# Where an expert's tokens sit among its slots, and the order of the last expert's loads and of the last sums

## The reference, cut to what matters

```python
scores = sigmoid(x @ w_router)                  # 544 x 64
idx = top_k(group_limited(scores + b_router), 6)
wts = scores[idx] / sum(scores[idx]) * 2.5
routed[token] += wts * (silu(x @ w_gate[e]) * (x @ w_up[e])) @ w_down[e]
shared = (silu(x @ ws_gate) * (x @ ws_up)) @ ws_down
out = layer_norm(ALPHA * x + routed + shared)
```

## Time and profile before

| | |
|---|---|
| median of 3 executions | 1910.4 us |
| the profiled execution, its own time | 1910.4 us |
| its span, first to last instruction | 1908.6 us |
| mean granted TensorE clock | 0.964 |
| TensorE busy | 1764.4 us, 92% of the span |
| VectorE / ScalarE / GpSimd busy | 748.9 / 552.0 / 346.0 us |
| moved by DMA | 358.60 MB |

### The profile page before, as it was taken

The page is one execution under the profiler, slowest core; times in us unless marked ns, Lnnn a source line. Parts: engine busy times, 40 slices in busy tenths (PEclk is TensorE's granted clock), DMA queues, the critical chain, the costliest instruction groups (busy, mean ns, idle before and its releaser), DMA issues. The chain is left out here.

```text
span 1908.6 us, 26693 instructions
## 1 busy us (share of the span) xinstructions
PE 1764.4 (92%) x10107; PEld 1168.1 (61%) x10107; DVE 748.9 (39%) x1853; ACT 552.0 (29%) x1293; POOL 346.0 (18%) x360
## 2 busy tenths in 40 slices
PE   8999999999999989899888788998999888899987
PEld 6577777777777768788666655565444344344432
DVE  1044544454554310265887443264222222222215
ACT  2134234233333321365667333020111111111110
POOL 0011211211211120031554262001111111111100
PEclk9999999999999989899799899999999999999999
DMA  7061221231232243153000365806999999999968
GB/s 234 1 215 47 64 75 47 57 82 47 57 73 54 46 118 95 45 177 94 14 2 1 133 214 186 302 26 274 364 421 420 420 420 419 419 421 419 419 272 321
DMA packets 165360, 358.60 MB, mean 188 GB/s; under 512 B 36920, under 2 KB 114736, under 8 KB 140400
## 3 DMA queue, kind: packets, MB, share of 16 engines
q1 hardware_dynamic: 144880, 295.33, 42.1%
q0 software_dynamic: 19872, 60.31, 8.9%
q10 hardware_dynamic: 480, 1.25, 0.2%
HBM read 337.75 MB, written 35.31 MB: 195 GB/s over the span
## 5 line engine op out<-in xcount | busy, mean ns | idle before, releaser
L848 PE MATMUL bank<-xT,arena 128*128 128x272 f32 x1440 | 373.1, 397 | 0.0
L848 PEld LDWEIGHTS bank<-xT,arena 128*128 128x128 f32 x1440 | 256.8, 190 | 58.1 <-issue 16.8
L2726 PE MATMUL bank<-arena,kvt 128*64 128x512 f32 (+1 forms) x816 | 263.9, 624 | 30.8 <-issue 29.9
L2726 PEld LDWEIGHTS bank<-arena,kvt 128*64 128x64 f32 (+1 forms) x816 | 89.9, 150 | 167.3 <-issue 167.3
L1265 POOL TENSOR_TENSOR arena<-arena 128x512 f32<-128x512 f32 x48 | 56.7, 1182 | 435.7 <-DVE arena L1355 261.3
L2805 PE MATMUL bank<-arena,kvt 128*64 128x512 f32 (+1 forms) x408 | 128.1, 598 | 2.4 <-issue 2.1
L3126 DVE SCALAR_TENSOR_TENSOR kvt<-kvt,arena,bank 128x256 f32<-128x256 f32 x37 | 17.8, 480 | 259.2 <-ACT kvt L2916 259.2
L2726 PE MATMUL bank<-xT,kvt 128*64 128x512 f32 (+1 forms) x208 | 99.6, 635 | 11.2 <-issue 11.2
L2572 POOL DMA_INDIRECT hT<-x_rows,rows_i x37 | 37.6, 1017 | 375.0 <-DVE rows_i L3057 375.0
L2916 ACT ACTIVATE kvt<-bank 128x256 f32<-128x256 f32 x37 | 14.2, 384 | 296.5 <-PE bank L2726 296.5
L1621 PE MATMUL bank<-xT,arena 128*128 128x272 f32 x352 | 83.0, 400 | 8.6 <-PEq L163 8.6
(11 more groups left out here) (504 smaller groups left out, 2994.9 us busy)
## 6 DMA issues: line engine op xcount, KB each, us to landing
arena<-in_w_exp_gate SPq DMA_DIRECT2D x51, 1024.0 KB, 21.7
arena<-in_w_exp_up SPq DMA_DIRECT2D x51, 1024.0 KB, 25.5
arena<-in_w_exp_down SPq DMA_DIRECT2D x51, 1024.0 KB, 24.6
arena<-in_w_in SPq DMA_DIRECT2D x48, 512.0 KB, 5.3
kvt<-in_w_exp_down SPq DMA_DIRECT2D x13, 1024.0 KB, 24.3
xT<-in_w_exp_gate SPq DMA_DIRECT2D x13, 1024.0 KB, 22.7
xT<-in_w_exp_up SPq DMA_DIRECT2D x13, 1024.0 KB, 26.2
arena<-y_rows SPq DMA_DIRECT2D x9, 1024.0 KB, 18.5
```

Of the source, the lines that this page charges most:

```text
L848: last = mm(banks[2 * (i % 2) + half][:, 0:HALF], wh[blk % RING][:, k, :], xT[:, k, half * HALF:(half + 1) * HALF], start=(k == 0), stop=( ...
L2726: last = mm(banks[2 + 4 * (t % 2)][cols, :], xgT[:, k, cols], ewgu[i % EBUF][:, :, k], start=(k == 0), stop=(k == KD - 1))
```

## The change

Three things are changed.

1. The constants `places_one` and `places_pair` and their two loads are gone. `match` compares with `slots`, whose value at slot s is s + 1: the list numbers lie in the slots in order, and the empty slots are the last ones of each expert. The two waits on `r_in` count 112 instead of 144.
2. The loads of the last two experts: one wait (for the gate_up of turn 34), then gate of 62, gate of 63, up of 62, up of 63 on two semaphores, then one wait for `y_banked` and both down matrices. In the last turn TensorE computes all gate columns first, after waiting for the gate matrices alone, and then all up columns after waiting for the up matrices: 32 calls of 256 columns instead of 16 of 512.
3. The last sums: `shared_down(3)` is moved ahead of the first chunk, and `shared_down(4)` with its wait stands behind `add_rows(3)` instead of ahead of it.

```diff
-            sp.dma_start(places_one, io["places_one"]).then_inc(r_in, 16)
-            sp.dma_start(places_pair, io["places_pair"]).then_inc(r_in, 16)
...
-            both = [(i, bass.ds(sp.value_load(...), 1)) for i in (NE - 2, NE - 1)]
-            for i, which in both:
-                sp.wait_ge(gu_banked, TURN_OF[i - EBUF] + 1)
-                load_gate_up(sp, i, which)
-            for i, which in both:
-                sp.wait_ge(y_banked, TURN_OF[i - EBUF] + 1)
+            both = [bass.ds(sp.value_load(...), 1) for i in (NE - 2, NE - 1)]
+            sp.wait_ge(gu_banked, TURN_OF[NE - 1 - EBUF] + 1)
+            for m, (name, landed) in enumerate((("w_exp_gate", last_gate_in), ("w_exp_up", last_up_in))):
+                for i, which in zip((NE - 2, NE - 1), both):
+                    sp.dma_start(ewgu[i % EBUF][:, m], io[name][0, which].rearrange("o (p k) n -> p (o k) n", p=P)).then_inc(landed, 16)
+            sp.wait_ge(y_banked, TURN_OF[NE - 1 - EBUF] + 1)
+            for i, which in zip((NE - 2, NE - 1), both):
                 load_down(sp, i, which)
...
             def gate_up(t):
-                for _, i, _ in columns(t):
-                    pe.wait_ge(we_in[i % EBUF], 32 * (i // EBUF + 1))
+                if t < NTURN - 1:
+                    for _, i, _ in columns(t):
+                        pe.wait_ge(we_in[i % EBUF], 32 * (i // EBUF + 1))
...
+                if t == NTURN - 1:
+                    for m, landed in enumerate((last_gate_in, last_up_in)):
+                        pe.wait_ge(landed, 32)
+                        for k in range(KD):
+                            for _, i, cols in columns(t):
+                                last = mm(banks[2 + 4 * (t % 2)][cols, m * DE:m * DE + DE], xgT[:, k, cols], ewgu[i % EBUF][:, m, k], start=(k == 0), stop=(k == KD - 1))
...
-            for q in range(3):
+            for q in range(4):
                 shared_down(q)
             pe.wait_ge(sums_in, 16)
             add_sample()
-            add_rows(1)
-            shared_down(3)
-            add_rows(2)
-            pe.wait_ge(sum_saved, 2)
-            shared_down(4)
-            add_rows(3)
-            add_rows(4)
+            for q in range(1, NTILE):
+                if q == 4:
+                    pe.wait_ge(sum_saved, 2)
+                    shared_down(q)
+                add_rows(q)
...
-                    last = V.tensor_tensor(onehot[t % 2][:, :, cols], (places_pair if len(TURNS[t]) == 2 else places_one).rearrange(...).to_broadcast([P, NTILE, width]),
+                    last = V.tensor_tensor(onehot[t % 2][:, :, cols], slots[:, 0:width].rearrange(...).to_broadcast([P, NTILE, width]),
                                            pos[:, :, which].to_broadcast([P, NTILE, width]), ALU.is_equal)
```

More of the change, by code:

```diff
@@ L121, in shape_constants @@
     c["slots"] = np.broadcast_to(i + 1, (P, P)).astype(f)
[L122 to L125, removed]
     c["runs"] = np.broadcast_to(np.arange(NTILE * NE) % NE != 0, (P, NTILE * NE)).astype(f)
@@ L435, in build @@
         slots = d(P)
-        places_one = d(P)
-        places_pair = d(LIGHT)
         capb = d(NE)
@@ L2431, in build @@
         chunk_in = [sem(f"chunk_in{i}") for i in range(14)]
+        last_gate_in = sem("last_gate_in")
+        last_up_in = sem("last_up_in")
         sums_in = sem("sums_in")
@@ L2524, in _ @@
                 load_down(sp, i, which)
-            both = [(i, bass.ds(sp.value_load(order[0:1, RANKS[i]:RANKS[i] + 1], min_val=0, max_val=NE - 1), 1)) for i in (NE - 2, NE - 1)]
-            for i, which in both:
-                sp.wait_ge(gu_banked, TURN_OF[i - EBUF] + 1)
-                load_gate_up(sp, i, which)
-            for i, which in both:
-                sp.wait_ge(y_banked, TURN_OF[i - EBUF] + 1)
+            both = [bass.ds(sp.value_load(order[0:1, RANKS[i]:RANKS[i] + 1], min_val=0, max_val=NE - 1), 1) for i in (NE - 2, NE - 1)]
+            sp.wait_ge(gu_banked, TURN_OF[NE - 1 - EBUF] + 1)
[4 more added lines that the diff above has]
+            for i, which in zip((NE - 2, NE - 1), both):
                 load_down(sp, i, which)
@@ L2656, in logits @@
                 if t == 0:
-                    pe.wait_ge(r_in, 144)
+                    pe.wait_ge(r_in, 112)
                 for k in range(KD):
@@ L2723, in gate_up @@
                     pe.wait_ge(h_ready, t - 1)
-                for k in range(KD):
-                    for _, i, cols in columns(t):
-                        last = mm(banks[2 + 4 * (t % 2)][cols, :], xgT[:, k, cols], ewgu[i % EBUF][:, :, k], start=(k == 0), stop=(k == KD - 1))
+                if t == NTURN - 1:
[4 more added lines that the diff above has]
+                                last = mm(banks[2 + 4 * (t % 2)][cols, m * DE:m * DE + DE], xgT[:, k, cols], ewgu[i % EBUF][:, m, k], start=(k == 0), stop=(k == KD - 1))
+                else:
+                    for k in range(KD):
+                        for _, i, cols in columns(t):
+                            last = mm(banks[2 + 4 * (t % 2)][cols, :], xgT[:, k, cols], ewgu[i % EBUF][:, :, k], start=(k == 0), stop=(k == KD - 1))
                 last.then_inc(gu_banked, 1)
@@ L3046, in match @@
                     width = cols.stop - cols.start
-                    last = V.tensor_tensor(onehot[t % 2][:, :, cols], (places_pair if len(TURNS[t]) == 2 else places_one).rearrange("p (o s) -> p o s", o=1).to_broadcast([P, NTILE, width]),
+                    last = V.tensor_tensor(onehot[t % 2][:, :, cols], slots[:, 0:width].rearrange("p (o s) -> p o s", o=1).to_broadcast([P, NTILE, width]),
                                            pos[:, :, which].to_broadcast([P, NTILE, width]), ALU.is_equal)
@@ L3067, in _ @@
                 norm(t)
-            dve.wait_ge(r_in, 144)
+            dve.wait_ge(r_in, 112)
             step(V.tensor_copy(R[:, :, 0], tokens[:, :, 0:1].to_broadcast([P, NTILE, NE])))
```

## The result

The change makes the kernel slower by 1.0%: 1929.22 us (median of 6 executions, 1926.38 to 1931.8) against 1909.51 us before (6 executions, 1909.12 to 1912.25), a ratio of 1.0101 with the interval 1.0088 to 1.0113. The profiled execution took 1931.04 us; its span is 1929.2 us, 20.6 us more than the one before.

A forecast was written before the change was run, and what follows sets the result against it. The prediction took the DMA transfers to bound the expert turns; 18.4 + 1.9 + 0.3 + 0.3 + 0 = 20.9 us on a span of 1908.6, with 1.8 around it, gave 1931.3 us, range 1918 to 1938.

The forecast's parts named there:

- Part 1: Expert turns: slots in order keep one DMA engine's eight slots filled, so turn 35 starts 18.4 us later.
- Lower bound 14.0, eight neighbours: Slot order, expert turns: if each engine serves eight neighbouring partitions, 14.0 us; within the smaller-imbalance rival, chance 0.10.
- Colder clock in turn 35: Turn 35's gate_up: a longer wait before it brings a slower clock and 9.0 us, +1.9 us, bounds 0 and 3.0.
- Part 2: Last two experts' loads and split gate_up: at most a 0.34 us wait saved, gate_up 7.10 to 7.8; taken +0.3 us.
- leaves no hole: Later issue of the last experts' loads: the queue still holds 11.4 us of work, so no delay.
- Last scatter: Scatter before the reading back: 7 rows on the fullest engine instead of 5, +0.3 us.
- Part 3: Reordered last sums: the wait before VectorE's group 4 only changes owner, 0 us, bounds -1.3 and +1.
- The signs: Expected traces: full-stretch share about 0.97, about 400 GB/s, gate_up waits up 15 to 20 us, weights landing in 22 us or more.
- Common limit: Rival, expert turns: memory limits all engines together, full ones speed up when light ones idle; 1912.5 us, chance 0.04.
- nothing: Rival, gathers and scatters: share-out is not by partition, so slot order does nothing; 1910.4 + 0.3 us, chance 0.02.
- faster: Rival, gathers and scatters: rows dealt one slot at a time, fullest engine falls by 15.4 us; 1895 us, chance 0.03.
- More: Rival, end of expert turns: turn 36's later loads meet an empty queue or cold clocks add up; +3 to +8 us, chance 0.06.

The follow-up runs named there:

- e1: Kernel before with only the list numbers in slot order and both constants gone, loads and sums as before: 1931.88 us against 1910.83, ratio 1.0118.
- e4: Kernel before with other constants: every second group of four slots wants the lower half of the list, the others the upper: 1935.95 us, ratio 1.0133.
- e5: Kernel before with other constants: slots 0 to 31 of each 64 want the lower half of the list, the rest the upper: 1910.06 us, ratio 0.9994.
- e9: Kernel before with slots 0-3 and 32-35 of each 64 holding list numbers 1 to 8, others dealt evenly: 1925.28 us, ratio 1.0103.
- e12: Kernel before with slots 24-27 and 56-59 of each 64 always filled, others dealt evenly: 1930.43 us against 1906.93, one execution.
- e14: Kernel before with slots 16-19 and 48-51 of each 64 always filled, others dealt evenly: 1933.96 us against 1906.93, one execution.
- e6: Kernel before with list numbers in reversed order, so the empty slots come first: 1933.72 us, ratio 1.0143.
- e13: Kernel before with slots 28-31 and 60-63 of each 64 always filled, others dealt evenly: 1924.82 us against 1906.93, one execution.
- e10: Kernel before with the groups of four mirrored within each 32 slots in every second pair of experts: 1906.52 us, ratio 1.0004.

## Why the prediction was right

The median came at 1929.2 us, 2.1 below the forecast, and the term that carries the forecast came for its reason. That the total is so near is in part luck: of the 20.6 us in the profile 4.7 were lost before turn 1, where the change does nothing, and what lies behind turn 1 adds up to 15.9 us against 20.9 forecast. Point by point:

**Part 1, +18.4 at turn 35.** Measured 17.2 over the expert stretch (e1: 16.7). The step that carries it, 62 transfers with 8 full slots on one engine times 0.156 us for a row, was right in kind: fixed groups (e4 against e5), fullest engine alone (e9). Its size was 1.2 us too large. The 378 rows before were read from the drain, and the count gives the same; but what the base is remains open, since the even variants differ in their fullest engine and not in time. Against the count of 495 to 378, 117 rows, the 17.2 us make 0.147 us a row.

**The assumption that engines are alike** stood in that step unsaid, and it is wrong (e12, e14). It did no harm because the change fills slots 0 to 7 and leaves the slow groups less full, by my count 392 rows on the engine of 16 to 19 and 308 on that of 24 to 27. With the full slots at 24 to 27 the same sum would have fallen 7 us short.

**Lower bound 14.0, eight neighbours.** Refuted by e4 and e5. The two ideas put the changed kernel's fullest engine at the same rows (496 against 495), because the first 36 slots are full either way, and differ only in the base, 14.0 against 18.4 us; that is why the two ideas could be left side by side in the forecast, and why other edits were needed to tell them apart.

**Colder clock in turn 35, +1.9.** Not in the profiled execution: turn 34 was itself late there and the wait before turn 35 was 2.71 us, followed by 7.10. It is in e1 (3.86, then 9.88), e4, e6, e9, e12, e13 and e14, but also in e10, whose engines are even (3.18, then 10.10), so it does not hang on the longer wait alone. So the term is real in some executions and absent in others, and the medians can't be parted into it. The rule that it came from, a wait of 3.5 us and the next gate_up takes 8.5, was too sharp. In e10 a wait of 4.02 us came before a gate_up of 7.10, and in the kernel before one of 3.01 came before 8.78. In the kernel after a wait of 2.24 us came before a gate_up of 8.79, one of 3.25 before 10.04, and one of 2.71 before 7.10.

**Part 2, +0.3.** Measured -0.3 from turn 35 to turn 36 in the profile. SyncE's queue in the kernel after:

```profile
1839.12 0.34 SPq L2524 DMA_DIRECT2D arena<-in_w_exp_gate  x1
1839.65 0.33 SPq L2524 DMA_DIRECT2D xT<-in_w_exp_gate  x1
1840.08 0.38 SPq L2524 DMA_DIRECT2D arena<-in_w_exp_up  x1
1840.55 0.63 SPq L2524 DMA_DIRECT2D xT<-in_w_exp_up  x1
1844.84 0.81 SPq L552 DMA_DIRECT2D arena<-in_w_exp_down  x2
```

All four go after turn 34's gate_up, as described, and turn 36 does not suffer: the down product of turn 35 ends and gate_up starts at once, at 1860.48. But "leaves no hole" was wrong for the lightly loaded engines. They stood mostly idle before the four loads came, while turn 35 still waited for its weights from the full ones; in e1, which issues the loads of expert 62 earlier, they did not. The kernel after, then e1:

```profile
1832.00:1836.00 4.00, 4.00 (x20) 1.36 (x20) 0.64 (x1) 0.55 (x1) 1.01 (x1) 1.00 0.63 258
1836.00:1840.00 4.00, 4.00 (x23) 1.80 (x19) 0.48 (x1) 0.38 (x1) 0.00 (x0) 1.00 0.29 119
```

```profile
1832.00:1836.00 4.00, 3.66 (x16) 1.26 (x16) 0.07 (x1) 0.10 (x2) 0.00 (x0) 1.00 0.97 399
1836.00:1840.00 4.00, 0.25 (x2) 0.28 (x4) 0.62 (x1) 0.53 (x1) 0.99 (x1) 0.82 1.02 426
```

From 1840 to 1856 us the share in the kernel after is back at 0.99 to 1.02. The hole cost nothing that the stretch shows (+17.2 here, +16.7 in e1), since turn 35 waits for the full engines. The 0.34 us wait of the earlier trace rows is saved, as the working had it for a warm turn 35. The finer matmuls cost nothing: 6.92 us for 64 of them, against 7.10 for 32, so the range of 7.10 to 7.8 lay on the wrong side.

**Last scatter, +0.3.** Measured 3.49 us against 4.79, a gain of 1.3 in this pair of profiles; e1 with the same slots took 4.30. What drains ahead of it differs between the kernels, and one landing was too little to put 0.3 on.

**Part 3, 0.** Measured +0.5, within -1.3 to +1. The wait has changed its owner as described. VectorE in the kernel after, end of group 3 and start of group 4, against the earlier trace rows:

```profile
1915.98 1.28 DVE L3189 SCALAR_TENSOR_TENSOR arena<-arena 128x1024 f32<-128x1024 f32 x1
1919.87 1.41 DVE L3180 SCALAR_TENSOR_TENSOR arena<-arena,bank 128x512 f32<-128x512 f32 x2 [2.60 <-PE bank L2690]
```

Before, VectorE came last and TensorE had finished its sums; now VectorE is free 2.6 us early and waits for `add_rows(4)`, behind which stands `shared_down(4)`.

**The signs.** The share fell to 1.00, not to 0.97, and the rate to 409 GB/s, not 400. In 468 us the rate of 410 against 420 is 11 us of lost transfer; most of the other 6 of the 17.2 are lost between 1832 us and turn 35, in the hole shown above. Over the whole way from turn 1 to turn 35 the rate is 415 before and 402 here, which is 206 MB both times. In e1, without that hole, it is 407, or 208 MB: there over 2 MB more have been moved when turn 35 starts, and the delay is the same. So the total rate does not tell the loss. The longer drain that the prediction named can be seen in e1 and e9, where the share stays under 1.00 from 1844 to 1864 us, 20 us against 16. The waits ahead of gate_up were to grow by 15 to 20 us and grew by 9.8, from 40.7 (turn 1 to turn 35 before) to 50.5. The rest is in gate_up itself: over turns 1 to 34 its pieces in the chain sum to 254.0 us before and 261.1 after, +7.1, and ten of them instead of seven took 8.4 us or more. 9.8 and 7.1 make 16.9 of the 17.2. A late load is paid as a wait or as a slower product after one, and only the two together are the loss. The split changes from profile to profile: in e1 it is 14.1 us of waits and 2.7 of gate_up, in e9 16.2 and 1.1, so there the waits alone come near the sign that was named. The windows of three gate_ups of the kernel after show the granted clock, a mean over each (in the second it is 0.50 until 1747 us and 0.98 from there on), after waits of 2.15, 5.01 and 2.24 us:

```profile
1723.78:1730.87 7.09, 7.09 (x33) 2.58 (x33) 0.14 (x1) 0.00 (x0) 0.47 (x1) 1.00 1.00 399
1741.74:1751.50 9.76, 9.76 (x33) 3.23 (x33) 0.00 (x0) 0.00 (x0) 0.00 (x0) 0.72 1.00 413
1616.61:1625.40 8.79, 8.79 (x33) 3.19 (x33) 0.04 (x1) 0.00 (x0) 0.37 (x1) 0.81 0.99 398
```

And one sign was wrong outright. The gate loads were to land after 22 us or more; their median fell from 21.7 to 13.2, while the up loads rose from 25.5 to 26.2. Every uneven variant whose page has the number shows it (gate 10.4 to 14.9 us), every even one doesn't (20.7 to 22.5). It marks unevenness reliably, but what makes it is not explained.

**The rivals.** "Common limit" falls by e9 and by the drain, "nothing" by e1, "faster" by every uneven run. "More" did not happen: turn 36's loads found the light engines idle, as said, but they were issued 21 us ahead of their use.

## What to carry to other kernels

When DMA engines are the bound, count the rows of each engine, not of each transfer: a transfer costs what its fullest engine costs, and empty slots on the same partitions turn after turn add up (here 148 rows over the mean, 17 to 25 us). Spread the padding over all groups of four partitions, and stop there: once the groups are within about a tenth of their mean (318 to 378 rows around 348 before, by my count), evening them further bought nothing in three tries. To price such a change read one stretch between two fixed events in several executions, since the start of the stretch alone moved by 11 us between profiles.

## What the runs showed of the hardware

- Gathers and scatters are shared out by partition: one engine serves two groups of four, 32 apart (e4 +24.3 us, e5 0.0).
- The engines aren't equal under such a load, for a reason that stays open: with the same 496 rows, slots 0 to 3 cost 17.4 us, 28 to 31 17.6, 16 to 19 21.9 and 24 to 27 25.1 (one profile each).
- Engines with less to do don't make up for a full one: 413 GB/s with two full engines, 410 with four at 440 rows or more, where even loads give 420.
- TensorE's granted clock in one gate_up was 0.72 after a wait of 5.01 us, but 0.81 after one of 2.24 and 1.00 after one of 2.15; in e10 it was 1.00 after one of 4.02. The length of the wait just before does not settle it.
